# Moving the attention output's evacuation on ScalarE into the next step, and re-cutting one product on TensorE

## The reference, cut to what matters

```python
def one(qblk):                       # 128 queries
    s = jnp.einsum('bqhmd,bkhmd->bhmqk', qblk, k).astype(jnp.float32) * scale
    p = jax.nn.softmax(s, axis=-1)
    a = p[:, :, 0] - lam * p[:, :, 1]
    return jnp.einsum('bhqk,bkhe->bqhe', a.astype(v.dtype), v)
```

## Time and profile before

| | |
|---|---|
| median of 3 runs | 1738.33 us (1734.19 to 1738.93) |
| the profiled execution | 1738.93 us, its span 1737.1 us |
| PE busy | 1676.8 us (97% of the span) |
| PEld busy | 1458.9 us (84%) |
| DVE busy | 1051.9 us (61%) |
| ACT busy | 787.6 us (45%) |
| POOL busy | 765.5 us (44%) |
| chain that ended last | PE 89%, DVE 5%, DMA 2%, SP's queue 2%, ACT 1% |

### The profile page before, as it was taken

One profiled execution on the slowest core, in us unless ns is written; L12 is line 12 of the kernel. 1 busy time (PEld: TensorE's weight loads), 2 busy tenths in 40 slices (PEclk: granted clock), 3 DMA queues, 4 the chain that ended last, 5 costly groups with the idle time before them and its releaser, 6 DMA issues.

```text
span 1737.1 us, 25198 instructions
## 1 busy us (share of the span) xinstructions
PE 1676.8 (97%) x8526; PEld 1458.9 (84%) x8526; DVE 1051.9 (61%) x1397; ACT 787.6 (45%) x1655; POOL 765.5 (44%) x807
## 2 busy tenths in 40 slices
PE   3899999999999999999969999999999999999999
PEld 1688888889999999999858788888888888878889
DVE  2552878883242241342378998787888888665553
ACT  3652333331010010100068988888888888711110
POOL 0000888881000000000068999999999999700000
PEclk8899999999999999999989999999999999999999
DMA  9963232232020020123242214114211211154441
GB/s 364 279 218 112 77 109 95 106 122 76 33 90 32 31 80 26 43 65 96 62 114 69 90 30 112 31 34 87 59 33 32 63 32 50 70 202 174 170 152 47
DMA packets 132628, 163.71 MB, mean 94 GB/s; under 512 B 10592, under 2 KB 121184, under 8 KB 131680
## 3 DMA queue, kind: packets, MB, share of 16 engines
q1 hardware_dynamic: 127440, 158.61, 28.3%
q10 hardware_dynamic: 5136, 4.46, 0.8%
HBM read 112.95 MB, written 50.07 MB: 94 GB/s over the span
## 4 chain that ended last, share of the span: by engine, by line
PE 89%; DVE 5%; DMA 2%; SPq 2%; ACT 1%; issue 1%; ACTq 0%; DVEq 0%
PE ps L728 44%; PE ps L882 14%; PE ps L871 12%; PE ps L975 11%; PE ps L863 6%; DVE stt L1606 2%; PE ps L792 2%; DMA scr<-in_xT 1%; PE ps L955 1%; DVE e L1588 1%; DVE wo L1573 0%; DMA scr<-in_xtok 0%; SPq L358 0%; SPq L371 0%; ACT e L1228 0%
## 5 line engine op out<-in xcount | busy, mean ns | idle before, releaser
L728 PE MATMUL ps<-hT,w 128*128 128x448 f32 (+1 forms) x3360 | 690.6, 365 | 0.0
L728 PEld LDWEIGHTS ps<-hT,w 128*128 128x128 f32 x3360 | 621.6, 188 | 62.4 <-issue 11.5
L1606 DVE TENSOR_REDUCE stt<-ps 128x1 f32<-128x1024 f32 x256 | 312.3, 1220 | 97.1 <-PE ps L882 94.3
L882 PE MATMUL ps<-kb,qb 128*128 (+1 forms) x1280 | 335.2, 392 | 12.9 <-ACT e L1228 6.5
L1228 ACT ACTIVATE e<-ps,stt 128x1024 f32<-128x1024 f32 x256 | 285.4, 1115 | 98.3 <-DVE stt L1606 97.6
L871 PE MATMUL ps<-at,vb 128*128 128x256 f32 x1088 | 276.5, 380 | 0.6 <-ACT atto L1185 0.5
L684 POOL TENSOR_TENSOR stt<-stt,lamc 128x2 f32<-128x2 f32 x64 | 12.5, 195 | 528.1 <-DVE stt L1631 528.1
L882 PEld LDWEIGHTS ps<-kb,qb 128*128 128x128 f32 x1280 | 206.4, 193 | 43.0 <-ACT e L1228 8.1
L871 PEld LDWEIGHTS ps<-at,vb 128*128 128x128 f32 x1088 | 201.0, 190 | 38.4 <-issue 1.3
L690 POOL TENSOR_TENSOR e<-e,stt 128x512 f32<-128x512 f32 (+1 forms) x192 | 209.2, 1090 | 5.0
L1139 ACT ACTIVATE scr<-ps 128x448 f32<-128x448 f32 (+1 forms) x40 | 20.9, 532 | 353.4 <-PE ps L728 353.4
(11 more groups left out here) (123 smaller groups left out, 1597.9 us busy)
## 6 DMA issues: line engine op xcount, KB each, us to landing
raw<-in_w_in SPq DMA_DIRECT2D x32, 512.0 KB, 4.0
qb<-spill_q SPq DMA_DIRECT2D x256, 64.0 KB, 2.3
scr<-in_xtok SPq DMA_DIRECT2D x8, 1024.0 KB, 8.0
wad<-in_w_ada SPq DMA_DIRECT2D x4, 2048.0 KB, 17.0
scr<-in_xT SPq DMA_DIRECT2D x8, 1024.0 KB, 6.6
spill_k<-scr SPq DMA_DIRECT2D x32, 224.0 KB, 2.2
spill_q<-scr SPq DMA_DIRECT2D x32, 224.0 KB, 2.2
mixc<-spill_cv SPq DMA_DIRECT2D x8, 896.0 KB, 8.9
```

Source lines behind the costliest of these rows:

```text
L728: mm = pe.matmul(out, slot_of(l, j), rhs_of(r, j), start=(i == 0 and j == 0), stop=(i == 2 and j == DJ - 1))
L882: mm = pe.matmul(out[:, c0 - k0:c1 - k0], qb[:, t, ver, m], keys, start=(ver == 0), stop=(ver == 1))
L1606: dve.tensor_reduce(stt[:, b, 0, 3 * m + c:3 * m + c + 1], ps[:, 2 * c:2 * c + 2, :].rearrange("p c n -> p (c n)"), AX.X, ALU.max, negate= ...
```

## The change

PE: the even step's 9 product matmuls are cut 0, 1, 4, 4 over the parts 0 to 3 (before 2, 2, 2, 3); the waits ahead of the even step's product move to part 1 with its first matmul. The odd step keeps 2, 2, 2, 2. ACT: `att_out` leaves part 3 of the odd step (where it waits for the product of that same step) and stands at the head of part 0 of the even step behind it; `att_store` follows in part 0. The indices of the waits and of the stored tile follow, and the drain after step 63 is rewritten to the same order. No work is added or removed.

```diff
-S_COMB, S_TR, S_PV, S_OUT = 1, 2, 4, 5
+S_COMB, S_TR, S_PV, S_OUT = 1, 2, 4, 6
...
             def product(b, half, part):
-                cut = (0, 2, 4, 6, 9) if half == 0 else (0, 2, 4, 6, 8)
+                cut = (0, 0, 1, 5, 9) if half == 0 else (0, 2, 4, 6, 8)
...
-                        if p == 0:
+                        if p == 1 - half:
                             pe.wait_ge(s_v[half], (32 if half else 16) * ((it + 3) // 4))
                             if half == 0:
                                 pe.wait_ge(t_act, 4 * (n - 3) + 3)
...
             def att_out(it, t):
-                pb = t // 2
-                act.wait_ge(pv_mm, 4 * it + t + 1 - S_PV)
-                wait(act, att_stored[pb], 16 * (it - 1))
+                pb = 1 if t == 0 else 0
+                act.wait_ge(pv_mm, 4 * it + t - S_PV)
+                wait(act, att_stored[pb], 16 * (it - (2 if t == 0 else 1)))
...
             def att_store(it, t):
-                pb = t // 2
-                act.wait_ge(att_evac, 2 * it - 1 + pb)
-                u = it - 1
+                pb = 1 if t == 0 else 0
+                act.wait_ge(att_evac, 2 * it - (2 if t == 0 else 1))
+                u = it - (2 if t == 0 else 1)
...
                 for p in range(4):
                     m, c = p // 2, p % 2
+                    if out and p == 0:
+                        att_out(it, t)
...
-                    if out and p == 3:
-                        att_out(it, t)
...
-                    if out and p == 3:
+                    if out and p == 0:
                         att_store(it, t)
...
-                    step(it, t, out=t % 2 == 1)
-            step(ITS, 0, sc=False, out=False, after=True)
+                    step(it, t, out=t % 2 == 0)
+            step(ITS, 0, sc=False, after=True)
...
             step(ITS, 1, sc=False, out=False, scale=False)
-            att_out(ITS, 1)
-            step(ITS, 2, sc=False, tr=False, out=False, scale=False)
-            att_store(ITS, 1)
-            att_out(ITS, 3)
-            att_store(ITS, 3)
+            step(ITS, 2, sc=False, tr=False, scale=False)
+            step(ITS + 1, 0, sc=False, tr=False, tr_last=False, scale=False)
```

More of the change, by code:

```diff
@@ L1277, in _ @@
                     n = 4 * it + t
-                    step(it, t, tr=n >= S_TR, tr_last=n > S_TR, out=n >= S_OUT and t % 2 == 1, scale=n >= 1)
+                    step(it, t, tr=n >= S_TR, tr_last=n > S_TR, out=n >= S_OUT and t % 2 == 0, scale=n >= 1)
                     if n == 1:
```

## The result

The changed kernel takes 1768.67 us (median of 4 runs, 1765.53 to 1769.89), the kernel before beside it 1736.49 us (4 runs, 1734.19 to 1738.93): 32 us slower by these medians. All 13 recorded runs of the changed kernel lie between 1761.34 and 1769.89 us; over them the ratio is 1.017 with a 95% interval of 1.0149 to 1.019, 26 to 33 us or about 1.7% slower. Forecast were 1775 us and a range of 1757 to 1786.

The account below looks back on a forecast made before the run. PE, full from 1080 to 1480 us, was taken as the bound. Steps 14 to 62 cost 30.7 us, step 6 1.6, steps 8 to 12 3.6, the drain 0.4: 36.3 on 1738.9 us, so 1775; range 1757 to 1786.

Parts of the forecast that it names:

- PE full, nothing to win, only waits to be made: Steady attention stage, 1080 to 1480 us: PE busy 400 of 400 us, so the edit can only add PE waits.
- First wait: Even step, scores of p = 1: PE waits 0.44 us for the odd step's last exponential, exposing a weight load.
- the bound by rows: Lower bound if only the wait ahead of the p = 1 scores counted: 0.77 us a step, 22 us, 1761.
- Second wait (g4's copy), t = 0: Ctx scores in even steps with t = 0: PE has no room, so the whole 1.29 us is lost.
- Second wait, t = 2: Ctx scores in even steps with t = 2: waiting for g4's copy, PE gains only 0.12 us, cost 1.17.
- Steps 8 to 13: Steps 8, 10 and 12: existing weight-load idle of 0.43 takes part of the owed work; 1.2 each, 3.6 us.
- I see nothing that recovers the loss: Parts 2 and 3 and the following odd step: the time lost in an even step is not given back later.
- Steps 5 to 7: Step 6: ACT's w_out cast stands ahead of att_out, which delays the exponential fully; 1.29 + 0.33 = 1.6 us.
- Step 4: Step 4 costs nothing, since PE arrives late there anyway, at a low clock.
- Step 63 and the drain: Drain: ACT is on the path between L1248 and the copies, and att_out enters it; 0.4 us.
- `att_evac` and `att_out` leaving part 3: att_out leaving the odd step's part 3 gives nothing; PE's att_evac wait, 0.5 us in all, stays covered.
- The clock: Rival: PE's idling in every even step lowers its clock, 44 us more, about 1819; chance 0.03.

Follow-up runs that it names:

- Experiment 6: Kernel before with the even step's product cut 2, 0, 3, 4 and ACT's g4 copy ahead of the exponential of p = 0: 1737.58 against 1735.64 us.
- experiment 1: Kernel before with only PE's even-step cut and waits changed (0, 1, 4, 4), ACT as before: 1761.51 against 1735.10 us.
- experiment 2: Changed kernel with PE's cut and waits as before (2, 2, 2, 3), so only ACT's move remains: 1798.30 against 1735.10 us for the kernel before.
- Experiment 4: Changed kernel with ACT's g4 copy ahead of the exponential of p = 0: 1756.04 against 1735.10 us for the kernel before.
- experiment 7: Kernel before with even-step cut 0, 2, 3, 4, the product's waits in part 1, g4's copy first: 1754.01 against 1734.01 us.
- experiment 3: Kernel before with even-step cut 1, 2, 3, 3, ACT as before: 1747.33 against 1735.10 us.

## Why the prediction was right, and where its sizes were off

- **PE full, nothing to win, only waits to be made.** Shown. Experiment 6 moves two products at almost no cost (0.17 and 0.02 a step) once both waits are out of the way, and experiments 1 and 2 show that neither edit wins anything. The earlier trace rows leave out one wait that the edit touches: PE waited for L1228 too, 4.1 us in three waits, all ahead of 892 us, in the start-up.
- **First wait (exponential of the odd step's last piece).** Shown, in place and in size: with it alone the loss is 0.78 to 0.84 us (experiments 4 and 7) where the bound by rows was 0.77, and it depends on what stands ahead of the scores of p = 1. The reading inside it was not right: "1.19 us against 0.93" set a record of the timeline against a share of the chain, which starts at the end of the group before. The record is 1.17 long in the unbroken row too. What is lost is the early start of 0.24 us behind transposes, nearly the same 0.26; that an uncovered weight load is its cause is not shown.
- **Second wait (g4's copy), t = 0.** Shown for the three products, 1.29 forecast and 1.30 measured; taking it away gives 0.52 back.
- **Second wait, t = 2.** The mechanism was right, and the term mis-sized: 1.17 forecast, 0.99 measured. I set the load of the ctx scores 2.27 us behind the accumulator read; it came 2.02 behind it. One part is the release: 0.51 us from the start of g4's copy came from a row of a step with t = 0, where it is 0.51 again in the changed kernel, but with t = 2 it is 1144.71 - 1144.32 = 0.39. The other part is ACT's overlap: `att_out` started 0.28 behind the read and not 0.32, the exponential 0.26 behind it and not 0.33, and g4's copy 1.09 behind that and not 1.11. Of 0.40 us for this wait 0.15 remained. 13 steps make 2.3 us.
- **Steps 8 to 13.** 3.6 forecast, 0.8 measured. I took one idle time of 0.43 off the owed 1.62. But in the kernel before these steps last 10.5 us against 9.7 of the steady ones, and 77% of the chain that ended last from 940 to 961 us is DVE's. So PE has some 0.8 us to spare in each of the two steps of a pair, and I had counted 0.43 once. Steps 8, 10 and 12 lost 0.4 to 0.5 us each, and the odd step behind each gave 0.2 back. "I see nothing that recovers the loss" holds only where PE has no idle time at all. Experiments 4 and 7, without the second wait, lose nothing in these steps.
- **Steps 5 to 7.** 1.6 forecast, 1.2 measured.
- **Step 4.** Forecast 0, and nothing is lost from step 3 to step 5.
- **Step 63 and the drain.** 0.4 forecast, 0.7 measured up to L1202 of step 64, and the step of the forecast holds: ACT's move makes it. Experiment 4, which has the move, loses 0.70 there too; experiment 1, which has not, -0.01. From L1248 to the next L1202 ACT takes 3.59 us instead of 2.87. Of the 0.72, 0.27 is `att_out` ahead of g4's copy; then ACT idles 0.31 us ahead of the copy of g0, where the program issues `att_store`, which I had put at nothing.
- **`att_evac` and `att_out` leaving part 3.** As forecast, neither won anything; that the re-cut has to come with ACT's move, or each even step stands 1.7 us behind the copy (experiment 2), was only implied in it.
- **The clock.** It did not fall: 1.00 from 1080 to 1480 us with PE idle for 13 us in 30 pieces, and 1.00 too in experiment 2, with 31 us in 19 pieces of up to 1.7. Both have short idles between groups of matmuls, over and over, and the oscillation that the Trainium skill reports for another kernel ("TensorE: Matmul & The Clock Gate", section "A second HAM failure mode: psum-queue depth-cycling") does not show in this one.

The sum was 36.3 us against 29.9 between the two profiled spans: 3.5 of the excess lie in steps 14 to 62, 2.8 in steps 8 to 13, 0.4 in steps 5 to 7, and the drain takes 0.3 off again. 2.3 of the 3.5 are the second wait with t = 2. So the mechanism was right and the sum a fifth too high; both its large errors go the same way, and no luck of opposite errors made the forecast.

## What to carry to other kernels

When an engine is full, an edit that only re-orders its list can lose and not win, and what it loses is read from the waits that the moved work was covering: list for each instruction behind the moved ones what it waits for, and when that is ready. Two waits in a row do not add up; the one that ends last counts. Here the second costs 1.30 us a step with t = 0 when both are there, and removing it gives back 0.52, because the first one still holds 0.78. Slack is a property of a stretch: where another engine sets the pace (steps 8 to 13), three even steps lost 0.8 us in all, and where PE never idled, each kept its 1.0 to 1.3 to the end. And a marker that is used to count, like L1202, must not itself change its place inside the step: in step 4 it did.

## What the runs showed that I had not expected

- The first step of a round differs from the others by some tenths, and it decides which wait ends last: DVE's maximum of p = 0 starts 0.45 us late in both steps with t = 0 that are shown, and the release of a waiting weight load from the start of the same ACT copy takes 0.51 us with t = 0 and 0.39 with t = 2. That this is the loop's boundary is argued from the program's order, not shown.
- A wait takes from PE the 0.24 us by which the group behind transposes starts early, on top of its own length, so a wait of hardly any length still costs: experiment 3, where PE came 0.07 us too early by the rows, lost 0.38 a step with t = 2 without any idle time on PE.
- The loss of a kind of step repeats to 0.04 us in the changed kernel, while the profiled executions differ by several microseconds ahead of step 5.
